# Projections of tile pairs in two delta-rule layers as 2x2 block products with seven block multiplications in f32

## The reference

```python
p = h @ w_in                      # (768 x 1024) @ (1024 x 6208)
qkv = silu(centred_dwconv(p[..., :4096], conv_w))    # q, k: 8 heads of 128, v: 16 heads of 128
z = p[..., 4096:6144]                                # gate, 16 heads of 128
```

## Time and profile before

| what | value |
|---|---|
| time, three runs | 3249.88, 3255.62, 5628.62 us, median 3255.62 |
| the profiled execution | span 3251.1 us; no other time of it is given |
| TensorE busy | 3092.5 us, 95% of the span |
| VectorE, ScalarE, GpSimd busy | 53%, 47%, 27% |
| mean granted TensorE clock | 0.978 of full |
| two slots (odd and even) of layer 0, 441.24 to 565.79 us | 124.55 us |
| two slots of layer 3, 2564.29 to 2676.02 us | 111.73 us |

### The profile page before, as it was taken

One profiled execution on the slowest core, in us unless ns is written; L12 is line 12 of the kernel. 1 busy time (PEld: TensorE's weight loads), 2 busy tenths in 40 slices (PEclk: granted clock), 3 DMA queues, 4 the chain that ended last, 5 costly groups with the idle time before them and its releaser, 6 DMA issues. The chain is left out here.

```text
span 3251.1 us, 55663 instructions
## 1 busy us (share of the span) xinstructions
PE 3092.5 (95%) x21673; PEld 2016.4 (62%) x21673; DVE 1731.2 (53%) x3543; ACT 1539.1 (47%) x3296; POOL 873.2 (27%) x652
## 2 busy tenths in 40 slices
PE   5889999999999999999999999897999999999998
PEld 3357777777777764455445555444777777777753
DVE  1156666666666652244443334346676767776632
ACT  3155555555555531256432444335655565555521
POOL 0044434533533410011001101003544435343400
PEclk9699999999999999999999999898999999999999
DMA  9921111211211126022311111102212222121135
GB/s 375 330 68 54 56 56 55 67 56 45 72 56 51 45 89 235 1 68 64 128 33 31 29 46 52 72 4 80 66 53 69 59 60 63 57 68 53 43 120 192
DMA packets 224097, 261.93 MB, mean 81 GB/s; under 512 B 19418, under 2 KB 158948, under 8 KB 223716
## 3 DMA queue, kind: packets, MB, share of 16 engines
q1 hardware_dynamic: 223844, 258.46, 24.7%
HBM read 239.15 MB, written 19.27 MB: 79 GB/s over the span
## 5 line engine op out<-in xcount | busy, mean ns | idle before, releaser
L898 PE MATMUL ps<-hT,W 128*128 128x512 f32 (+1 forms) x2656 | 1001.2, 506 | 3.0 <-DVEq L192 2.0
L898 PEld LDWEIGHTS ps<-hT,W 128*128 128x128 f32 x2656 | 470.5, 193 | 195.1 <-issue 165.6
L1331 DVE CAST_PREDICATED arena<-mask,ps 128x384 bf16<-128x384 uint32 x448 | 253.2, 565 | 223.2 <-PE ps L967 174.3
L1148 ACT CAST arena<-ps 128x384 bf16<-128x384 f32 x384 | 166.9, 482 | 347.7 <-PE ps L954 346.7
L2372 PE MATMUL ps<-arena 128*128 128x512 f32 x712 | 311.2, 595 | 2.3 <-SPq L192 2.0
L1333 DVE CAST_PREDICATED arena<-mask,ps 128x384 bf16<-128x384 uint32 x448 | 250.9, 560 | 0.0
L2372 PEld LDWEIGHTS ps<-arena 128*128 128x128 f32 x712 | 134.5, 191 | 167.1 <-issue 162.8
L2007 PE MATMUL ps<-hT,W 128*128 128x512 f32 (+1 forms) x608 | 218.2, 493 | 0.6 <-DMA W<-in_att_w_in 0.4
L1455 POOL TENSOR_TENSOR arena<-arena 128x768 f32<-128x768 f32 (+1 forms) x32 | 44.4, 1389 | 636.0 <-ACT arena L1192 636.0
L1268 DVE SCALAR_TENSOR_TENSOR arena<-arena,vec 128x770 f32<-128x770 f32 (+1 forms) x192 | 205.4, 1070 | 6.8
L967 PEld LDWEIGHTS ps<-arena 128*128 128x128 bf16 x2304 | 144.7, 98 | 55.4 <-issue 51.0
(11 more groups left out here) (284 smaller groups left out, 6177.0 us busy)
## 6 DMA issues: line engine op xcount, KB each, us to landing
arena<-in_ada_w SPq DMA_DIRECT2D x24, 2048.0 KB, 19.5
W<-in_gdn_w_in SPq DMA_DIRECT2D x95, 512.0 KB, 4.0
arena<-decay_sums SPq DMA_DIRECT2D x64, 384.0 KB, 4.1
W<-decay_rows SPq DMA_DIRECT2D x64, 384.0 KB, 5.0
arena<-in_gdn_w_out SPq DMA_DIRECT2D x32, 512.0 KB, 10.5
W<-in_gdn_w_out SPq DMA_DIRECT2D x30, 512.0 KB, 3.4
arena<-gated SPq DMA_DIRECT2D x32, 384.0 KB, 7.7
gated<-arena SPq DMA_DIRECT2D x24, 384.0 KB, 2.3
```

The lines of the kernel that those rows point to most:

```text
L898: mm = pe.matmul(ps[:, b, 0:t1 - t0], w[:, i, :], env.hT[:, i, t0:t1], start=(i == 0), stop=(i == KD - 1))
L1148: act.copy(half_cols(Xb[d], s, d), ps[:, 2 * d, 0:384].rearrange("p (c b s) -> p c b s", c=NT, s=s)).then_inc(*inxe.up(m, lv, d))
L1331: dve.copy_predicated(half_cols(Mb[d], s, d), wide(env.m4[:, d, lv]), src_m).then_inc(*inm.up(m, lv, d, "m"))
```

## The change

Two tiles that stand one below the other (k and the q of the same head, called A; v and z of a unit, called B) are now one 2x2 block product. The tiles' K = 1024 is cut in halves (4 matmuls each), the columns of `hT` in halves `H0` and `H1` of 384 (256 in layer 3). Seven block products 1 to 7 replace eight: each is a use of 4 matmuls of 384 columns. The first operands of products 3 to 7 are sums of blocks of the weights, which GpSimd forms for each pair (four operations of 512 columns), in `W` itself and in `ksum2`, `vsum1`, `vsum2` and a part of `x`. The second operands are three sums of blocks of `hT`, which GpSimd forms at the phase's start (1536 columns each) and keeps in `x`. The sums of the results are made where a use is taken out: A1, A6, B1, B6, B5, B3 are copied by ScalarE, and A2, A5, A3, A7, A4, B2, B7, B4 are taken out by VectorE with an addition (`add`). Six uses (`CHAIN`) go on in the bank of another one without clearing it, once that one was taken out. In layer 3 the context columns of k and v stay plain products (c0, c1).

With it: SiLU of z is one operation of its own at the end of a slot (`gates`), SiLU of v moves from p = 14 to 15, A1 and A6 of the next k/q pair stand at the end of odd slots, q has a weight tile of its own, the cosine, sine and band tables move from the constants into the attention phase's arena, and `x` is loaded again (two DMAs, 3 MB) at the end of slot 14; before layer 3 it is first stored.

Cut to its core:

```diff
+CHAIN = {"A6": "A1", "A4": "A7", "B6": "B1", "B5": "B6", "B3": "B5", "B4": "B7"}
+ON_DVE = ("A2", "A5", "A3", "A7", "A4", "B2", "B7", "B4")
 def fill(n, use, i, steps):
     if starts and prev:
-        pe.wait_ge(aev.sem, aev.at(*prev))
+        kept = dev if prev[1] in ON_DVE else aev
+        pe.wait_ge(kept.sem, kept.at(*prev))
-    if use[0] in "XVZ":
+    if use[0] in "AB":
+        mm = strassen(n, use, i, ps[:, b, 0:HALF])
...
+def strassen(n, use, i, o):
+    w, x = {1: (first[:, i], env.hT[:, i, H0]), 2: (first[:, KD2 + i], env.hT[:, KD2 + i, H0]),
+            3: (first[:, KD2 + i], env.hT[:, KD2 + i, H1]), 4: (second[:, KD2 + i], h4[:, i]),
+            5: (sum1[:, i], env.hT[:, i, H1]), 6: (sum2[:, i], h2[:, i]), 7: (second[:, i], h3[:, i])}[which]
+    return pe.matmul(o, w, x, start=(i == 0 and use not in CHAIN), stop=(i == KD2 - 1), ...)
...
+def add(n, use):                                     # VectorE
+    dve.wait_ge(ad.sem, ad.at(n, use))
+    src, m = ps[:, before[n, use][0], 0:HALF], n + 1
+    if use == "A5":
+        dve.tensor_tensor(kw, ku, src, ALU.add).then_inc(*dev.up(n, use))
+    elif use in ("B7", "B4"):
+        dve.tensor_tensor(v.sz[:, m % 2, H1 if use == "B7" else H0], vw if use == "B7" else vu, src, ALU.add)...
+    else:                                            # A2, A3, A7, A4, B2 into pad
+        for to, of in pieces(H1 if use in ("A3", "A7") else H0):
+            ins = dve.tensor_tensor(pad[:, to], more, src[:, of], ALU.add)
 # VectorE, end of each position, behind conv, finish and nrm
+for use in done[n, p]:
+    if use in ON_DVE:
+        add(n, use)
 # GpSimd, start of a slot
+pool.tensor_tensor(s1, za, zb, ALU.add).then_inc(*bform.up(m, 1))
+pool.tensor_tensor(s2, s1, va, ALU.subtract).then_inc(*bform.up(m, 2))
+pool.tensor_tensor(za, va, za, ALU.subtract).then_inc(*bform.up(m, 3))
```

## The result

The changed kernel takes **3505.8 us** (median of 4 runs, 3502.9 to 3508.7) against 3249.9 us for the kernel before on the same chip, the median of its three fast runs (a fourth, in the slow state, took 5628.6 us and is not compared): ratio **1.0791, 95% interval 1.0772 to 1.0811**. The profiled execution spans 3506.9 us at a mean granted clock of 0.957 (before: 3251.1 us and 0.978). Forecast were 3340 us and 3250 to 3390. The direction was right, the size was not: about +256 us where the forecast has +89.

A forecast was written before the change was run, and what follows sets the result against it. TensorE, busy 95% of the span, was taken as the bound. 93 us less work against 180 us of new waits: 3251.1 + 14 x 6.7 - 4 + 1 = 3342, given as 3340 us, range 3250 to 3390.

The forecast's parts named there:

- GpSimd's 15 us more in two slots run beside VectorE: GpSimd's added work slows VectorE's predicated copies by 7% at most: 1 us in two slots, 14 in all, within the range.
- the rule: Trainium skill: GpSimd shares SBUF interfaces with VectorE and contends with its instructions of two SBUF inputs.
- are at 1.02 us in these slots: VectorE's convolution operations before the change, beside less GpSimd work than afterwards; cited against the skill's contention rule.
- The waits of VectorE's order: Layer 0: TensorE waits for late additions, B4 behind B7 3.2 and 3.3 us, A4 behind A7 2.2, B1 behind A5 1.35.
- My longest waits are 3.2 and 3.3: Layer 0's two waits of B4 behind B7, in us; a quarter shorter than the 4.4 us wait seen with lower clock.
- That rival: The clock drops as well: the longest waits slow TensorE about 3 us more each time, 84 us, giving 3425; chance 0.08.
- TensorE's saving: Matmuls at 0.64 us per 384 columns save 7.8 us (layer 0) and 4.9 (layer 3) in two slots, 93 us less work.
- the waits are covered: Rival: each addition is done before its bank is wanted, so the 93 us saving stays: 3158 us; chance 0.12.
- Weight DMAs and sums as releasers: Sign of being wrong: TensorE's waits are ended by GpSimd's sums or by a weight DMA.
- TensorE busy under 117: Sign for the forecast: two slots of layer 0 last 128 to 133 us with TensorE busy under 117.

The follow-up runs named there:

- E1: The change with GpSimd's weight sums one column wide (products then use weights that aren't summed), all waits kept: 3385.9 us, ratio 1.0437.
- E2: The change with GpSimd's weight sums moved to other places in its order, all work kept: 3463.2 us, ratio 1.0670.
- S1: The kernel before, with TensorE waiting behind V1 for a 1536-column GpSimd copy in odd slots: 3273.1 us, ratio 1.0076.
- S5: The kernel before, with TensorE waiting behind V1 for a 1536-column GpSimd copy in every slot: 3295.8 us, ratio 1.0171.
- S2: The kernel before, with TensorE waiting behind V1 for a 3840-column GpSimd copy in odd slots: 3321.9 us, ratio 1.0232.
- S3: The kernel before with one of eight contraction steps of every X, V and Z projection left out: 3188.6 us, ratio 0.9820.
- B2: The kernel before with an eighth of each X, V and Z projection left out and `capped` late in layer 3's odd slots: 3167.3 us, ratio 0.9772.
- E9: The change with one-column weight sums in both layers and VectorE's additions first in layer 0 alone: 3357.5 us, ratio 1.0340.
- E4: The kernel before with two-input GpSimd operations of 512 columns added at the places of the change's weight sums: 3343.8 us, ratio 1.0297.
- E3: The change with VectorE's additions for A7 and B7 placed first, GpSimd's order unchanged: 3483.6 us, ratio 1.0732.

## Why the prediction was wrong

*The step that failed* is the one on GpSimd: "GpSimd's 15 us more in two slots run beside VectorE ... 14 us in all". It took the predicated copies as a measure, one operand of which comes from PSUM; operations of VectorE that read only SBUF take turns with GpSimd's and last up to twice as long and more (the convolution's three 6.88 against 3.1 us). The forecast set the rule aside because the convolutions "are at 1.02 us in these slots": true of layer 0, where nothing lay beside them, so the row said nothing for or against. The row that decides (the 512-column convolution of layer 3) was in the trace and was not asked for. Measured: 133 us (E1; 120 between medians) where the sum had nothing and the range 14. In the slots of the change no wait of TensorE was ended by a sum, and of 0.7 us at most by another operation of GpSimd, so nearly all of it came by way of VectorE.

*The waits of VectorE's order* were right in kind and nearly in size: 6.0, 1.9 and 1.1 us against 6.5, 2.2 and 1.35 (E2, layer 0). E1, which has the order of the forecast and no sums to speak of, idles 15.3 us in two slots of layer 0 where the forecast had 16.1. Its slots are 6.9 us longer than forecast all the same (138.2 against 131.3), since TensorE is busy 122.8 us and not 123.7 - 7.8 = 115.9: up to 2.8 us of that is clock (0.98 of 138.1), and about 0.2 for each wait, which S1 and S5 measured, would bring most of the rest.

*The clock.* "My longest waits are 3.2 and 3.3" and so 0.08 for it. S2 shows that 3.5 us brings it about; in the change the waits are 3.4 to 4.8 us, and the clock costs up to 9.6 and 6.5 us in two slots. That rival's mechanism was there, mostly on top of contention (E1 keeps a clock of 0.98 in layer 0 with longest waits of 3.8 us), and its 3425 us are still 80 short of the result.

*TensorE's saving.* The price of a matmul was right: eight records of 384 columns, four matmuls, from 642.20 to the next at 644.78, are 0.645 us each against 0.64.

```profile
642.20 2.75 PE L952 MATMUL ps<-hT,W 128*128 128x384 f32 x8
644.78 0.51 PE L1032 MATMUL ps<-arena 128*128 128x64 bf16 x12
```

But 93 us less work need not become 93 us less time: S3 removes at least as much (7.7 and 6.5 us in two slots against 7.8 and 4.9; 95 matmuls of 512 columns and 72 of 256 in all, some 112 us) and gives 66 us between the profiled executions, 57 between the medians. In the order of the kernel before, the rival "the waits are covered", 3158 us, was therefore out of reach. B2, with `capped` moved, comes near it (span 3164.5 us); what the order of the change would allow was not tried.

*Weight DMAs and sums as releasers.* No wait of TensorE in the slots of the change was ended by a weight DMA or a sum; a sum ended one only where I moved `b_last` (1.7 us in E2). "TensorE busy under 117" was a bad mark: a slower clock and the ends of matmuls ahead of waits count as busy (125.6 us).

Against the forecast of 3342 us for the profiled execution the span is 165 us over: 133 are the sums (3506.9 to 3374.0), and 32 remain in E1. They lie in layer 0: from the first to the last start of the squares of the output E1 needs 82 us more than the kernel before where the forecast has 47, in layer 3 46 where it has 47. What they consist of, clock, the 0.2 us of each wait and `capped` beside the convolution, is argued from the windows, not shown. Additions first take 19 us back (3374.0 to 3355.0, E9), but those are waits that the forecast had. How the 133 divide into waits and clock is also read from the windows alone; no run holds the clock fixed.

## What to carry to other kernels

Before work is put on an idle GpSimd, lay its new operations beside VectorE's operations that read only SBUF and price every overlap as if the two ran one after the other; operations with an operand in PSUM kept their time here. What an overlap costs depends on who waits behind VectorE: 2.7 us in two slots of layer 0 in E4, 9.7 in the change. To see whether a kernel pays already, compare the same line in different shapes: an operation that takes longer in the smaller shape (1280 ns for 512 columns, 1040 for 770 in the kernel before) has something beside it. And an operation that waits for TensorE in GpSimd's queue also moves everything behind it, here `capped` into the convolution.

A saving on the engine that is 95% busy is first to be tried by itself, by leaving that much work out; here it gave 57 to 66 us for some 112 us of work, and the block products had to pay for additions, sums and longer waits out of about as much.

## What the runs showed of the hardware

- VectorE and GpSimd, both reading only SBUF, work nearly one at a time: three sums and four 768-column operations, 7.4 us alone, fill 6.8 us. So 768-column f32 operations of two inputs take 1.8 us instead of 0.95 and GpSimd's 512-column sums 1.8 to 2.0 instead of 1.27, and a one-column sum 0.91 instead of 0.19 (E1). A GpSimd copy of one input slows VectorE as much (1270 ns against 1274), and VectorE's operations with an operand in PSUM are not slowed (L1457, two in 1.81 us).
- A stall of TensorE of 1.6 us costs 1.8 us and leaves the clock at 1.00, also when there are two of them in two slots (S1, S5); a stall of 3.5 us costs 5.3 to 5.7, 1.7 of it clock (0.78 and 0.93 over the 12 us around its end, S2).
- Three kernels with different orders (the change, E2, E3) have 129.6 to 129.8 us for most pairs of slots in layer 3, with 15 to 17 us of idle time and a clock of 0.95. Why they meet at that value stays open.
